# Six expert weight blocks in flight instead of four, with large SBUF buffers laid out in multiples of 512 bytes

## The chip, the cores and the metric

The kernel runs on one core of one Trainium2 chip. The metric is device time of one execution in microseconds (us). Engines are named as in the profile: PE is TensorE (PEld its weight loads), DVE is VectorE, ACT is ScalarE, POOL is GpSimd, SP is SyncE, which issues most loads.

## The reference

Two small networks run one after the other on 256 tokens of width 1024, in float32. The last and longest part is a layer of eight experts of which each token takes two:

```python
def moe(h, router, wg, wu, wd):
    logits = (h @ router).astype(jnp.float32)
    vals, idx = lax.top_k(logits, TOP_K)
    w = jax.nn.softmax(vals, axis=-1)
    gates = jnp.sum(jax.nn.one_hot(idx, N_EXPERTS, dtype=jnp.float32) * w[..., None], axis=-2)
    y = jnp.zeros_like(h)
    for e in range(N_EXPERTS):
        y = y + gates[..., e:e + 1].astype(h.dtype) * swiglu(h, wg[e], wu[e], wd[e])
    return y
...
def first_block(x, ...):
    for i in range(DEPTH):
        h = h + (moba_attention if i == 0 else rwkv7_time_mix)(rms_norm(h, norm_mix[i]), ...)
        h = h + conv_ffn(rms_norm(h, norm_ffn[i]), ...)
    return rms_norm(h, norm_final)
```

The second network (second_block) has two layers, each with modulation from a vector c, a mixer of differential attention beside a gated linear recurrence, and then a feed-forward: dense in the first layer, the experts in the second.

## The kernel before

All big weight matrices are cut on the host into blocks of 128 partitions x 2048 float32 (1 MB, 8192 bytes a partition): 162 dense blocks in the order of use, then 36 blocks for each of the 8 experts, 288 in all. A block goes through three steps. SyncE loads it into one of the RING = 4 slots of `ring`. ScalarE rounds it to float32r into one of SPLITS = 3 slots of `weights_hi` (the semaphore `hi_ready`). VectorE subtracts the rounded from the original into `weights_lo` and counts up `taken`, which lets TensorE start on the block and lets SyncE load the next one into the ring slot. TensorE multiplies hi by hi, hi by lo and lo by hi, and counts up `used`, which frees the split slot for ScalarE. So each product takes three matmuls.

The activations are split in the same way into `acts_hi` and `acts_lo`. `to_features` (L735) has a piece of the weights as its stationary operand and 256 columns of acts as the moving one: 48 matmuls a block. `to_tokens` (L746) has acts stationary and 256 columns of weights moving, 48 matmuls a block; its 12 blocks are four of the first attention, four of RWKV and two of each mixer. `project` (L766) has acts, heads or hidden values stationary and 512 columns of weights moving, 24 matmuls a block. RWKV has eight blocks of to_features and four of to_tokens.

The order on each engine is written by hand and unrolled for the dense part. The experts are a loop of seven passes and a last pass. In a pass TensorE takes six chunks of gate and up blocks (L2771, twelve 512-column matmuls a block, `xg_hi` and `xg_lo` stationary), each followed by four transposes (L2789) and two down blocks (L2814, `hT_hi` and `hT_lo` stationary). Near the end of a pass it gathers the tokens of the next expert (L2742), and near the start it scatters the results of the last one (L2754, L2756). On ScalarE `moe_hi` (L2261) rounds, on VectorE `moe_lo` (L2267) subtracts, on SyncE `load` (L2730) issues. The first four expert blocks are issued by `issue` (L340), the function of the dense ones, during the last mixer, under its wait that four blocks back has been taken.

Before the experts the router runs (L3035 to L3072): small steps between TensorE and VectorE, in which VectorE does the lower half of expert block 1 in two parts. At the very start of the kernel POOL loads the positions and the four lambda vectors; `rope_angles` and `products` on VectorE use them.

Buffers are given addresses in the order in which the program asks for them, in steps of 32 bytes, and given back at the end of a stage. Ahead of `ring` lie 16,384 bytes and four small constants in 32-byte steps, so in each partition `ring` begins at 16,512, `weights_hi` at 49,280 and `weights_lo` at 73,856, all 128 bytes past a multiple of 512. Below, the residue of a buffer is its start modulo 512. Before the change `acts_hi` begins at 153,088 (residue 0) up to the first feed-forward, at 188,064 (160) in RWKV, and at 144,896 (0) from the second feed-forward on; `hid_hi_part` has residue 0, `ada` 0, `xg_hi` and `hT_hi` 192. Each lo buffer has the residue of its hi buffer. The address table of the change follows from the sizes in the diff: a slot of `ring` is 8192 bytes, `resid`, `xn` and `AT` 8192 each, `seen` 2048.

Of the kernel before, what the change touches and what calls it, by code (L numbers as in the profile page):

```python
# [15 lines left out]
P = 128  # L16
T = 256
# [6 lines left out]
RING = 4  # L24
SPLITS = 3
# [86 lines left out]
VCOLS = _at  # L112

# [31 lines left out]
def expert_order():  # L145

    order = []
    for c in range(CHUNKS + 1):
        if c < CHUNKS:
            order += [("gate", c, 0), ("gate", c, 1), ("up", c, 0), ("up", c, 1)]  # L150
        if c:
            order += [("down", c - 1, 0), ("down", c - 1, 1)]
    assert len(order) == EXPERT_BLOCKS and EXPERT_BLOCKS % RING == 0 and EXPERT_BLOCKS % SPLITS == 0
    return order
# [59 lines left out]
def build(nc, a, out):  # L214
# [6 lines left out]
    with ExitStack() as ctx:  # L221
# [40 lines left out]
        stat = sb("stat", [P, 64])  # L262
# [7 lines left out]

        arrived = [sem(f"arrived{i}") for i in range(RING)]
        hi_ready = sem("hi_ready")
# [525 lines left out]
        seen = sb("seen", [P, TT, T])  # L798
        nlam = sb("nlam", [P, 2])
        decay8 = sb("decay8", [P, 8])  # L800
        pos_in = sem("pos_in")
# [23 lines left out]
        posq = sb("posq", [P, TT], I32, stage=heads_stage)  # L825
        fl = sb("fl", [P, 4, T], stage=heads_stage)
        cq = sb("cq", [P, TT], stage=heads_stage)
        lams = sb("lams", [P, 4, 2, DH], stage=heads_stage)
        dots = sb("dots", [P, 2, 2], stage=heads_stage)
        sp8 = sb("sp8", [P, 6, 8], stage=heads_stage)  # L830

        stages = open_joint()
        with ExitStack() as stage:
            x_in = sem("x_in")
            early_in = sem("early_in")
            norm = Norm(lambda f: v("norm_mix", f), turns=0, then=0, look=1, joined=False)
            no = norm.no
            ahead(SPLITS)
            with engine_programs() as block:
                @block.sync  # L840
                def _(sp):
                    sp.dma_start(cst[:, 0:EARLY], a["consts"][:, 0:EARLY]).then_inc(early_in, 16)
                    sp.dma_start(resid[:], a["x"][0].rearrange("(t p) d -> p t d", p=P)).then_inc(x_in, 16)
                    feed(sp, 3)
                    sp.dma_start(cst[:, EARLY:ROPE], a["consts"][:, EARLY:ROPE]).then_inc(cst_in, 16)
                    feed(sp, 5)
                    sp.dma_start(cst[:, ROPE:], a["consts"][:, ROPE:]).then_inc(cst_rest, 16)
                    feed(sp)

                @block.gpsimd  # L850
                def _(pool):
                    pool.dma_start(posb[:], a["positions_2"][0:1, :].broadcast_to([P, T])).then_inc(pos_in, 16)
                    pool.dma_start(posq[:], a["positions_2"][0].rearrange("(t p) -> p t", p=P), allow_slow_non_contiguous=True).then_inc(lams_in, 16)
                    for i, n in enumerate(("lam_q1_2", "lam_k1_2", "lam_q2_2", "lam_k2_2")):
                        pool.dma_start(lams[:, i, :, :].rearrange("p l d -> p (l d)"),
                                       a[n].rearrange("(a l) d -> a (l d)", a=1).broadcast_to([P, 2 * DH])).then_inc(lams_in, 16)

                @block.scalar
                def _(act):
                    act.dma_start(vec[:], a["vectors"]).then_inc(setup_in, 16)  # L860
# [36 lines left out]
        with ExitStack() as stage:  # L897
# [6 lines left out]
            PT += [own_PT[:, i] for i in range(2)]  # L904
            st = sb("st", [P, 8, 2, 6], stage=stage)
            heads = [sb(n, [P, KT, T], F32R, stage) for n in ("heads_hi", "heads_lo")]
# [10 lines left out]
            with engine_programs() as block:  # L917
# [129 lines left out]
                def _(dve):  # L1047
# [5 lines left out]
                    def rope_angles():  # L1053

                        dve.wait_ge(pos_in, 16)
# [99 lines left out]
                    for i in range(12):  # L1155
# [5 lines left out]
                        if i == 0:  # L1161
                            dve.wait_ge(cst_in, 16)
                            dve.wait_ge(lams_in, 80)
                            products()
# [1053 lines left out]
        open_acts(ctx)  # L2218
# [31 lines left out]
        m_xhi, m_xlo, m_hlo, m_oh, m_gc, m_st = (sem("m_" + n) for n in ("xhi", "xlo", "hlo", "oh", "gc", "st"))  # L2250
# [4 lines left out]

        def moe_hi(act, n, j):

            slot = (moe_first + j) % RING
            act.wait_ge(arrived[slot], n * (16 * EXPERT_BLOCKS // RING) + 16 * ((moe_first + j) // RING + 1))
            act.wait_ge(used, n * EXPERT_BLOCKS + (moe_first + j - SPLITS + 1))  # L2260
            nc.scalar.copy(split[0][:, (moe_first + j) % SPLITS, :], ring[:, slot, :]).then_inc(hi_ready, 1)  # L2261

        def moe_lo(dve, n, j, lo=0, hi=BLK):

            at = (moe_first + j) % SPLITS
            dve.wait_ge(hi_ready, n * EXPERT_BLOCKS + (moe_first + j + 1))
            ins = nc.vector.tensor_tensor(split[1][:, at, lo:hi], ring[:, (moe_first + j) % RING, lo:hi],  # L2267
                                          split[0][:, at, lo:hi].bitcast(F32), ALU.subtract)
            if hi == BLK:
                ins.then_inc(taken, 1)  # L2270
            else:
                dve_step.mark(ins)

        Q0, K0, X0, X1, Q1, K1, Y0, Y1, V0, V1 = range(10)
        ROTATED = (Q0, K0, Q1, K1)

        def mixer(l, no, then, norm):
# [7 lines left out]
            with ExitStack() as stage:  # L2285
                QK = sb(f"QK{l}", [P, 8, T], stage=stage)
                V = sb(f"V{l}", [P, TT, 512], stage=stage)
                xp = sb(f"xp{l}", [P, 4, T + 3], stage=stage)
# [10 lines left out]
                st = sb(f"st{l}", [P, 4, 2, 3, TT], stage=stage)  # L2299
                Pd = sb(f"Pd{l}", [P, 2, 2 * T], stage=stage)  # L2300
                PT = sb(f"PT{l}", [P, 2, 2 * T], stage=stage)
                O = raw[:].rearrange("p t (h n) -> p t h n", h=4)
# [383 lines left out]
        make_gates(1)  # L2686
        norm = Norm(gain_of(1, 0), shift(1, 0), turns=6, then=first["win1"], look=2)
        ffn(2, no, first["win1"], norm, scale=gates[0][:, 1, :], finished=1)
        router, rgain, rshift = (sb(n, [P, KT, EXPERTS]) for n in ("router", "rgain", "rshift"))
        rbias = sb("rbias", [P, EXPERTS])  # L2690
# [4 lines left out]
        slot_no = sb("slot_no", [P, 2, TT, EXPERTS])  # L2695
        gate_w = sb("gate_w", [P, TT, EXPERTS])
        info = sb("info", [1, 3 * EXPERTS], I32)
        yacc = sb("yacc", [P, TT, D])
        E = EXPERTS
        lg = sb("lg", [P, TT, E])  # L2700
        w3 = [sb(f"w3_{i}", [P, TT, E]) for i in range(5)]
        riota = sb("riota", [P, E])
        m = sb("m", [P, 8, TT])
        cn = sb("cn", [P, 4, E])
        with ExitStack() as stage:
# [3 lines left out]
            gcol = sb("gcol", [P, TT, 1], stage=stage)  # L2709
# [4 lines left out]
            oe = [sb(z, [P, D], F32R, stage) for z in ("moe_hi", "moe_lo")]  # L2714
            first_use = {key: j for j, key in enumerate(order)}
# [263 lines left out]
            with engine_programs() as block:  # L2979
                @block.sync  # L2980
                def _(sp):
                    with sp.Fori(0, E - 1) as e:
                        for j in range(RING, EXPERT_BLOCKS):
                            load(sp, e, e, j)
                        for j in range(RING):
                            sp.wait_ge(taken, e * EXPERT_BLOCKS + (EXPERT_BLOCKS + moe_first + j - RING + 1))
                            src = expert_block(e + 1, j)
                            slot = (moe_first + j) % RING
                            sp.dma_start(ring[:, slot, :], src).then_inc(arrived[slot], 16)
                    for j in range(RING, EXPERT_BLOCKS):  # L2990
# [26 lines left out]
                def _(act):  # L3017
# [8 lines left out]
                    nc.scalar.copy(ST[:].rearrange("p (a b) -> p a b", a=2), zeros(2, P)).then_inc(m_st, 1)  # L3026
# [106 lines left out]
```

## Time and profile before

| | |
|---|---|
| median of 3 runs | 2150.48 us (2148.81 to 2155.33) |
| the profiled execution | 2152.8 us, its span 2151.0 us |
| TensorE busy | 97% of the span |
| VectorE, ScalarE busy | 81%, 59% |
| mean granted TensorE clock | 0.981 of full speed |
| experts (1258.7 to about 2133 us of the span) | 288 blocks of 1 MB |
| mean HBM rate | 248 GB/s over the span, about 350 in the experts |

Busy time of TensorE is modelled at its end: matmuls overlap, so one of 512 columns shows about 395 ns though the next starts some 233 ns later. The distance from start to start, or the length of a chain piece over its count, is what tells the pace. Idle time of an engine costs only where the chain of waits passes through it.

### The profile page before, as it was taken

To read this page: it belongs to the slowest core of one execution; us is meant where nothing else is said; L and a number is where in the kernel's file an instruction comes from. 1 tells how busy PE (TensorE), PEld (TensorE's weight loads), DVE (VectorE), ACT (ScalarE), POOL (GpSimd) and SP (SyncE) were. 2 spreads that over 40 slices of the span, in tenths; PEclk is the share of its full clock that TensorE was granted. 3 is DMA by queue.
4 is the path that set the end of the run, shared out by engine and by line. 5 is a ranking of instruction groups with operands and counts; after the bars stand their busy time and mean duration, and the time that the engine had idled before them with its cause. 6 is when DMAs were issued, how large, how long until landed. Compare 5 with 4: busy or idle time off the path is not lost.

```text
span 2151.0 us, 31960 instructions
## 1 busy us (share of the span) xinstructions
PE 2087.0 (97%) x12604; PEld 1784.4 (83%) x12605; DVE 1734.9 (81%) x1995; ACT 1260.7 (59%) x1272; POOL 47.9 (2%) x83
## 2 busy tenths in 40 slices
PE   8999999998999999999999999999999999999996
PEld 7889996877789979799988878888888888888885
DVE  7758887796688878778788778988888888888886
ACT  5654444632354455753345777777677777777774
POOL 0000001000000000000000000000000000000000
PEclk9999999998799999999999999999999999999998
DMA  7358861201377644387864349898989898989894
GB/s 258 128 189 281 298 232 63 105 21 41 130 262 262 251 158 160 115 301 296 298 251 143 126 184 361 332 363 326 357 329 365 325 368 321 366 327 355 346 360 178
DMA packets 79070, 534.09 MB, mean 248 GB/s; under 512 B 11648, under 2 KB 13056, under 8 KB 15216
## 3 DMA queue, kind: packets, MB, share of 16 engines
q1 hardware_dynamic: 71440, 481.04, 60.0%
q0 software_dynamic: 7376, 51.25, 6.5%
q8 instruction: 78, 1.28, 0.2%
q14 instruction: 32, 0.26, 0.0%
q10 hardware_dynamic: 144, 0.26, 0.0%
HBM read 531.47 MB, written 1.05 MB: 248 GB/s over the span
## 4 chain that ended last, share of the span: by engine, by line
PE 86%; DVE 7%; ACT 3%; DMA 2%; issue 1%; SPq 0%; DVEq 0%; ACTq 0%
PE bank L735 25%; PE bank L2771 23%; PE bank L766 12%; PE bank L2814 11%; PE bank L746 3%; DMA ring<-in_experts 1%; PE bank L2742 1%; PE bank L409 1%; DVE weights_lo L2267 1%; PE bank L2789 1%; DVE weights_lo L373 1%; ACT weights_hi L365 1%; ACT weights_hi L2261 1%; DVE AT L2096 1%; DVE S L2095 1%
## 5 line engine op out<-in xcount | busy, mean ns | idle before, releaser
L2267 DVE TENSOR_TENSOR weights_lo<-ring,weights_hi 128x2048 fp32r<-128x2048 f32 x289 | 657.8, 2283 | 100.2 <-ACT weights_hi L2261 97.2
L2261 ACT CAST weights_hi<-ring 128x2048 fp32r<-128x2048 f32 x288 | 550.6, 1915 | 160.3 <-PE bank L2771 60.7
L735 PE MATMUL bank<-acts_hi,weights_hi 128*128 128x256 f32 x1600 | 458.1, 286 | 8.2 <-DVE acts_lo L395 4.3
L373 DVE TENSOR_TENSOR weights_lo<-ring,weights_hi 128x2048 fp32r<-128x2048 f32 x162 | 370.3, 2290 | 111.6 <-ACT weights_hi L365 110.1
L365 ACT CAST weights_hi<-ring 128x2048 fp32r<-128x2048 f32 x162 | 308.9, 1909 | 251.0 <-PE bank L735 224.2
L735 PE MATMUL bank<-acts_hi,weights_lo 128*128 128x256 f32 x1600 | 452.1, 283 | 0.0
L735 PE MATMUL bank<-acts_lo,weights_hi 128*128 128x256 f32 x1600 | 450.7, 282 | 0.0
L735 PEld LDWEIGHTS bank<-acts_hi,weights_hi 128*128 128x128 f32 x1600 | 302.0, 189 | 17.5 <-issue 12.9
L2771 PE MATMUL bank<-weights_hi,xg_hi 128*128 128x512 f32 x768 | 308.4, 402 | 1.0 <-DVE xg_lo L2890 0.4
L735 PEld LDWEIGHTS bank<-acts_lo,weights_hi 128*128 128x128 f32 x1600 | 302.2, 189 | 2.7 <-issue 1.4
L2771 PE MATMUL bank<-weights_hi,xg_lo 128*128 128x512 f32 x768 | 303.7, 395 | 0.0
L2771 PE MATMUL bank<-weights_lo,xg_hi 128*128 128x512 f32 x768 | 303.5, 395 | 0.0
L735 PEld LDWEIGHTS bank<-acts_hi,weights_lo 128*128 128x128 f32 x1600 | 301.4, 188 | 0.0
L2771 PEld LDWEIGHTS bank<-weights_hi,xg_hi 128*128 128x128 f32 x768 | 144.3, 188 | 36.4 <-DVE weights_lo L2267 2.8
L2771 PEld LDWEIGHTS bank<-weights_hi,xg_lo 128*128 128x128 f32 x768 | 144.4, 188 | 35.0
L2771 PEld LDWEIGHTS bank<-weights_lo,xg_hi 128*128 128x128 f32 x768 | 144.5, 188 | 32.3
L2814 PE MATMUL bank<-weights_hi,hT_hi 128*128 128x512 f32 x384 | 121.5, 398 | 1.8 <-DVE hT_lo L2931 1.8
L2814 PE MATMUL bank<-weights_hi,hT_lo 128*128 128x512 f32 x384 | 120.7, 395 | 0.0
L2814 PE MATMUL bank<-weights_lo,hT_hi 128*128 128x512 f32 x384 | 120.7, 395 | 0.0
L1383 DVE CUSTOM_DVE_ANT_0 ada<-ada,silu_c 128x1024 f32<-128x1024 f32 x96 | 113.5, 1220 | 0.8 <-ACT silu_c L1327 0.8
L766 PE MATMUL bank<-weights_hi,hid_hi_part 128*128 128x512 f32 x272 | 89.6, 403 | 1.5 <-DVE hid_lo_part L1370 1.5
L766 PE MATMUL bank<-weights_lo,hid_hi_part 128*128 128x512 f32 x272 | 87.4, 395 | 0.0
(467 smaller groups left out, 2743.7 us busy)
## 6 DMA issues: line engine op xcount, KB each, us to landing
ring<-in_experts SPq DMA_DIRECT2D x288, 1024.0 KB, 5.4
ring<-in_dense SPq DMA_DIRECT2D x162, 1024.0 KB, 4.9
ada<-in_ada POOLq DMA_DIRECT2D x48, 1024.0 KB, 5.1
silu_c<-in_c SPq DMA_DIRECT2D x3, 512.0 KB, 6.2
resid<-in_x SPq DMA_DIRECT2D x1, 1024.0 KB, 6.7
out<-resid SPq DMA_DIRECT2D x2, 512.0 KB, 2.6
cst<-in_consts SPq DMA_DIRECT2D x1, 649.5 KB, 9.9
kh<-in_rwkv_g SPq DMA_DIRECT2D x1, 512.0 KB, 7.1
```

The costliest lines, as they stand in the source:

```text
L365: nc.scalar.copy(split[0][:, n % SPLITS, :], ring[:, n % RING, :]).then_inc(hi_ready, 1)
L373: nc.vector.tensor_tensor(split[1][:, n % SPLITS, :], ring[:, n % RING, :], split[0][:, n % SPLITS, :].bitcast(F32), ALU.subtract).then_in ...
L409: nc.tensor.matmul(pb[bank][:], ident, const("cos", 0, 2 * T), start=True, stop=True)
L735: ins = nc.tensor.matmul(bank[:, f * T:(f + 1) * T], split[w][:, m % SPLITS, k * 256 + f * P:k * 256 + (f + 1) * P], acts[x][:, k, :], sta ...
L746: ins = nc.tensor.matmul(bank[:, t * 256:(t + 1) * 256], acts[x][:, k, t * P:(t + 1) * P], split[w][:, m % SPLITS, k * 256:(k + 1) * 256], ...
L766: ins = nc.tensor.matmul(pb[4 + 2 * t + h][:], src[x][:, tile + f, t * P:(t + 1) * P], split[w][:, m % SPLITS, f * D + h * 512:f * D + (h ...
L1383: ins = nc.vector.tensor_tensor_reduce(out=w, in0=w, in1=silu_c[:], op0=ALU.mult, op1=ALU.add, scale=1.0, scalar=0.0, accum_out=mods[:, l, ...
L2095: L(tt(o, N[:, w:, j:w].broadcast_to([P, n, w]), Z[:, j:w, 0:w].broadcast_to([P, n, w]), ALU.mult))
L2261: nc.scalar.copy(split[0][:, (moe_first + j) % SPLITS, :], ring[:, slot, :]).then_inc(hi_ready, 1)
L2267: ins = nc.vector.tensor_tensor(split[1][:, at, lo:hi], ring[:, (moe_first + j) % RING, lo:hi], split[0][:, at, lo:hi].bitcast(F32), ALU.s ...
L2771: ins = nc.tensor.matmul(bank[:], xp[x][:, 4 * half + k, :], split[w][:, slot, k * 512:(k + 1) * 512], start=(half == 0 and k == 0 and w + ...
L2814: ins = nc.tensor.matmul(pb[6 + b][:], hT[x][:, c % 2, q * P:(q + 1) * P], split[w][:, slot, f * D + b * 512:f * D + (b + 1) * 512], start ...
```

## The change

Six blocks are in flight in the experts. The two new ring places, `ring_more`, lie where the split activations lay, which are given back after the last mixer; SyncE loads into them once TensorE has used the last dense block. `place(j)` gives the buffer and the semaphore of block j: its index modulo DEEP = 6, the first four in the old ring, two in the new one. The small tensors (constants, vectors, statistics, router terms) are gathered into a few pieces, `small`, `few`, `routing` and `kept`, whose sizes are multiples of 512 bytes, and buffers of odd size come last in their stage. `make_gates(1)` takes its memory earlier. The semaphores `pos_in` and `m_st` are dropped: their instructions count on `lams_in` and `m_oe`, and the waits are raised to match.

```diff
 RING = 4
+MORE = 2
+DEEP = RING + MORE
...
+SMALL = 2944
...
-        mods = sb("mods", [P, 2, 48])
-        gain2 = sb("gain2", [P, 2, 2, KT])
-        cst = sb("cst", [P, CONSTS.shape[1]])
-        vec = sb("vec", [P, VCOLS])
         resid = sb("resid", [P, TT, D])
         xn = sb("xn", [P, TT, D])
         AT = sb("AT", [P, KT, T])
-        stat = sb("stat", [P, 64])
+        seen = sb("seen", [P, TT, T])
+        small = sb("small", [P, SMALL])
...
+        cst, vec, stat = piece(CONSTS.shape[1]), piece(VCOLS), piece(64)
+        mods = piece(96).rearrange("p (l n) -> p l n", l=2)
...
         posb = sb("posb", [P, T], I32, stage=heads_stage)
-        posq = sb("posq", [P, TT], I32, stage=heads_stage)
         fl = sb("fl", [P, 4, T], stage=heads_stage)
-        cq = sb("cq", [P, TT], stage=heads_stage)
         lams = sb("lams", [P, 4, 2, DH], stage=heads_stage)
-        dots = sb("dots", [P, 2, 2], stage=heads_stage)
-        sp8 = sb("sp8", [P, 6, 8], stage=heads_stage)
+        few = sb("few", [P, P], stage=heads_stage)
...
-                        dve.wait_ge(pos_in, 16)
+                        dve.wait_ge(lams_in, 96)
...
-        bonus = sb("bonus", [P, TT, HEADS], stage=rwkv)
         S0 = sb("S0", [P, KT, DH], stage=rwkv)
-        fac = sb("fac", [P, KT], stage=rwkv)
...
         make_gates(0)
-        open_acts(ctx)
+        make_gates(1)
+        routing = sb("routing", [P, 3 * P])
...
+        split_acts = ExitStack()
+        open_acts(split_acts)
...
+        def place(j):
+
+            i = j % DEEP
+            if i < RING:
+                slot = (moe_first + i) % RING
+                return ring[:, slot, :], arrived[slot], 16 * ((moe_first + i) // RING)
+            return ring_more[0][:, i - RING, :], arrived_more[i - RING], 0
+
         def moe_hi(act, n, j):
 
-            slot = (moe_first + j) % RING
-            act.wait_ge(arrived[slot], n * (16 * EXPERT_BLOCKS // RING) + 16 * ((moe_first + j) // RING + 1))
+            src, sem_in, earlier = place(j)
+            act.wait_ge(sem_in, n * (16 * EXPERT_BLOCKS // DEEP) + (earlier + 16 * (j // DEEP + 1)))
             act.wait_ge(used, n * EXPERT_BLOCKS + (moe_first + j - SPLITS + 1))
...
+        split_acts.close()
+        ring_more[0] = sb("ring_more", [P, MORE, BLK])
+        kept = sb("kept", [P, P])
...
             def load(sp, e, n, j):
 
-                src = expert_block(e, j)
-                slot = (moe_first + j) % RING
-                sp.wait_ge(taken, n * EXPERT_BLOCKS + (moe_first + j - RING + 1))
-                sp.dma_start(ring[:, slot, :], src).then_inc(arrived[slot], 16)
+                dst, sem_in, _ = place(j)
+                sp.wait_ge(taken, n * EXPERT_BLOCKS + (moe_first + j - DEEP + 1))
+                sp.dma_start(dst, expert_block(e, j)).then_inc(sem_in, 16)
...
                 if t == 0:
-                    pe.wait_ge(m_st, 1)
-                    pe.wait_ge(m_oe, s * 2 + 2)
+                    pe.wait_ge(m_oe, s * 2 + 3)
...
                 def _(sp):
+                    sp.wait_ge(used, moe_first)
+                    for j in range(RING, DEEP):
+                        dst, sem_in, _ = place(j)
+                        sp.dma_start(dst, expert_block(0, j)).then_inc(sem_in, 16)
                     with sp.Fori(0, E - 1) as e:
-                        for j in range(RING, EXPERT_BLOCKS):
+                        for j in range(DEEP, EXPERT_BLOCKS):
                             load(sp, e, e, j)
```

## Rows read from the trace of the kernel before

**Rows 1.** The page: busy time of TensorE, its granted clock, DMA by slices.
```profile
PE 2087.0 (97%) x12604; PEld 1784.4 (83%) x12605; DVE 1734.9 (81%) x1995; ACT 1260.7 (59%) x1272; POOL 47.9 (2%) x83
...
PEclk9999999998799999999999999999999999999998
DMA  7358861201377644387864349898989898989894
```

**Rows 2.** The chain that ended last, experts: start us, length us, what.
```profile
1359.82 3.57 PE bank L2742 x32
1363.39 5.60 PE bank L2814 x24
...
1387.88 0.44 PE bank L2789 x4
...
1468.92 3.57 PE bank L2742 x32
...
2015.84 3.57 PE bank L2742 x32
```

**Rows 3.** The same chain where it leaves TensorE, first stretch.
```profile
1536.88 7.60 DMA ring<-in_experts
...
1544.58 1.92 ACT weights_hi L2261
...
1546.53 2.30 DVE weights_lo L2267
```

**Rows 4.** Waits from 1250 us on: total us, times, longest us.
```profile
DVE weights_lo L2267 <- ACT weights_hi L2261: 97.2, 157, 1.6
...
ACT weights_hi L2261 <- DMA ring<-in_experts: 52.0, 56, 2.3
...
PEld bank L2771 <- DVE weights_lo L2267: 2.8, 6, 0.7
```

**Rows 5.** Timeline of SyncE and TensorE around the last projection: start us, us.
```profile
1234.02 0.36 SPq L2730 DMA_DIRECT2D ring<-in_experts  x1
...
1255.10 0.34 SPq L2730 DMA_DIRECT2D ring<-in_experts  x1
...
1240.05 0.39 PE L766 MATMUL bank<-weights_hi,acts_lo 128*128 128x512 f32 x1
```

**Rows 6.** Timeline of POOL and VectorE at the start, and the landings of lams.
```profile
4.26 0.57 POOL L855 DMA_DIRECT2D lams<-in_lam_k  x1
...
23.37 0.49 DVE L1083 TENSOR_TENSOR lams<-lams 128x128 f32<-128x128 f32 x2
...
DMA to landing us min/median/max: 7.1/7.6/9.0
```

**Rows 7.** Groups of VectorE by form: count, then busy us, mean ns of one.
```profile
L1370 DVE TENSOR_TENSOR hid_lo_part<-hf,hid_hi_part 128x512 fp32r<-128x512 f32 x34 | 23.5, 692 | 20.0 <-ACT hid_hi_part L1324 20.0
...
L395 DVE TENSOR_TENSOR acts_lo<-mix,acts_hi 128x512 fp32r<-128x512 f32 x12 | 7.5, 685 | 1.5 <-ACT acts_hi L389 1.5
```

**Rows 8.** The page's DMA issues: count, KB each, median us to landing.
```profile
ring<-in_dense SPq DMA_DIRECT2D x162, 1024.0 KB, 4.9
ada<-in_ada POOLq DMA_DIRECT2D x48, 1024.0 KB, 5.1
```

**Rows 9.** The chain in two dense feed-forward stretches.
```profile
206.79 11.52 PE bank L735 x96
218.31 5.58 PE bank L766 x24
...
1035.13 11.39 PE bank L735 x96
```

**Rows 10.** Timeline of TensorE in RWKV; 13 such rows lie between these.
```profile
366.27 0.28 PE L735 MATMUL bank<-acts_lo,weights_hi 128*128 128x256 f32 x1
...
367.91 0.28 PE L735 MATMUL bank<-acts_hi,weights_hi 128*128 128x256 f32 x1
```

**Rows 11.** The page's groups: to_features, one of its three operand pairs.
```profile
L735 PE MATMUL bank<-acts_hi,weights_hi 128*128 128x256 f32 x1600 | 458.1, 286 | 8.2 <-DVE acts_lo L395 4.3
```

More of the change, by code:

```diff
@@ L152, in expert_order @@
             order += [("down", c - 1, 0), ("down", c - 1, 1)]
-    assert len(order) == EXPERT_BLOCKS and EXPERT_BLOCKS % RING == 0 and EXPERT_BLOCKS % SPLITS == 0
+    assert len(order) == EXPERT_BLOCKS and EXPERT_BLOCKS % DEEP == 0 and EXPERT_BLOCKS % SPLITS == 0
     return order
@@ L261, in build, with piece @@
         AT = sb("AT", [P, KT, T])
-        stat = sb("stat", [P, 64])
+        seen = sb("seen", [P, TT, T])
+        small = sb("small", [P, SMALL])
+        at_small = [0]
+        def piece(n):
+            at_small[0] += n
+            assert at_small[0] <= SMALL
+            return small[:, at_small[0] - n:at_small[0]]
+        cst, vec, stat = piece(CONSTS.shape[1]), piece(VCOLS), piece(64)
+        mods = piece(96).rearrange("p (l n) -> p l n", l=2)
+        gain2 = piece(4 * KT).rearrange("p (l i k) -> p l i k", l=2, i=2)
+        nlam, decay8, fac = piece(2), piece(8), piece(KT)
+        bonus = piece(TT * HEADS).rearrange("p (t h) -> p t h", t=TT)
         def const(name, lo=0, n=None):
@@ L271, in build @@
         arrived = [sem(f"arrived{i}") for i in range(RING)]
+        arrived_more = [sem(f"arrived_more{i}") for i in range(MORE)]
         hi_ready = sem("hi_ready")
@@ L904, in build @@
             PT += [own_PT[:, i] for i in range(2)]
+            heads = [sb(n, [P, KT, T], F32R, stage) for n in ("heads_hi", "heads_lo")]
             st = sb("st", [P, 8, 2, 6], stage=stage)
-            heads = [sb(n, [P, KT, T], F32R, stage) for n in ("heads_hi", "heads_lo")]
             sc = DH ** -0.5
@@ L2217, in build @@
         make_gates(0)
-        open_acts(ctx)
+        make_gates(1)
+        routing = sb("routing", [P, 3 * P])
+        router, rgain, rshift = (routing[:, 64 * i:64 * i + 64].rearrange("p (k e) -> p k e", k=KT) for i in range(3))
+        rbias, riota = routing[:, 192:200], routing[:, 200:208]
+        by_tile = lambda i: routing[:, 208 + 16 * i:224 + 16 * i].rearrange("p (t e) -> p t e", t=TT)
+        lg, w3, m = by_tile(0), [by_tile(1 + i) for i in range(5)], routing[:, 304:320].rearrange("p (i t) -> p i t", t=TT)
+        cn = routing[:, 320:352].rearrange("p (i e) -> p i e", e=EXPERTS)
+        split_acts = ExitStack()
+        open_acts(split_acts)
         no = norm_turn(lambda f: v("norm_ffn", KT + f), turns=3, then=ffn_plan[1]["gate", 0], look=2)
@@ L2249, in build @@
         m_t, m_ht, m_oe, m_sc, m_y = (sem("m_" + n) for n in ("t", "ht", "oe", "sc", "y"))
-        m_xhi, m_xlo, m_hlo, m_oh, m_gc, m_st = (sem("m_" + n) for n in ("xhi", "xlo", "hlo", "oh", "gc", "st"))
+        m_xhi, m_xlo, m_hlo, m_oh, m_gc = (sem("m_" + n) for n in ("xhi", "xlo", "hlo", "oh", "gc"))
         routed = sem("routed")
@@ L2266, in moe_lo @@
             dve.wait_ge(hi_ready, n * EXPERT_BLOCKS + (moe_first + j + 1))
-            ins = nc.vector.tensor_tensor(split[1][:, at, lo:hi], ring[:, (moe_first + j) % RING, lo:hi],
+            ins = nc.vector.tensor_tensor(split[1][:, at, lo:hi], place(j)[0][:, lo:hi],
                                           split[0][:, at, lo:hi].bitcast(F32), ALU.subtract)
@@ L2272, in moe_lo @@
                 dve_step.mark(ins)
+        ring_more = [None]
         Q0, K0, X0, X1, Q1, K1, Y0, Y1, V0, V1 = range(10)
@@ L2714, in build @@
             oe = [sb(z, [P, D], F32R, stage) for z in ("moe_hi", "moe_lo")]
+            gcol = sb("gcol", [P, TT, 1], stage=stage)
             first_use = {key: j for j, key in enumerate(order)}
@@ L2981, in _ @@
                 def _(sp):
+                    sp.wait_ge(used, moe_first)
+                    for j in range(RING, DEEP):
+                        dst, sem_in, _ = place(j)
+                        sp.dma_start(dst, expert_block(0, j)).then_inc(sem_in, 16)
                     with sp.Fori(0, E - 1) as e:
-                        for j in range(RING, EXPERT_BLOCKS):
+                        for j in range(DEEP, EXPERT_BLOCKS):
                             load(sp, e, e, j)
[L2985 to L2990, printed above, removed]
+                        for j in range(DEEP):
+                            dst, sem_in, _ = place(j)
+                            sp.wait_ge(taken, e * EXPERT_BLOCKS + (EXPERT_BLOCKS + moe_first + j - DEEP + 1))
+                            sp.dma_start(dst, expert_block(e + 1, j)).then_inc(sem_in, 16)
+                    for j in range(DEEP, EXPERT_BLOCKS):
                         load(sp, E - 1, E - 1, j)
@@ L3025, in _ @@
                         nc.scalar.copy(z[:].rearrange("p (a b) -> p a b", a=2), zeros(2, D // 2)).then_inc(m_oe, 1)
-                    nc.scalar.copy(ST[:].rearrange("p (a b) -> p a b", a=2), zeros(2, P)).then_inc(m_st, 1)
+                    nc.scalar.copy(ST[:].rearrange("p (a b) -> p a b", a=2), zeros(2, P)).then_inc(m_oe, 1)
                     all_passes(act, act_pass)
```

35 lines of the change are left out of this document (13 added, 22 removed).

## The prediction

> **What bounds the kernel now.** I read the page first: TensorE is busy for 97% of the span, and in the second half, where the experts run, the 16 DMA engines alternate between 8 and 9 tenths of busy time [rows 1]. So either TensorE or the weight stream could be the limit of the part that the ring change aims at, and the shares don't say which. The chain of waits does. It runs through the experts on TensorE alone, with pieces of 24 matmuls in 5.60 us (two weight blocks, so 2.80 us a block), except in two stretches, near 1530 and near 1955, where it goes round a loop of weight DMA, ScalarE rounding and VectorE subtraction [rows 2, 3]. Waits say what that is worth. ScalarE waits for a landing 56 times, 52.0 us in all; VectorE waits for ScalarE for 97.2 us; but TensorE's weight loads wait for VectorE's lower halves only 6 times, 2.8 us in total [rows 4]. SyncE issues each load as soon as VectorE frees its slot, so the slots set when it starts. So the loads are often late for ScalarE and almost never for TensorE, and TensorE's queue is what ends last.
>
> The length of a pass confirms it. Gathers start at 1359.82 and 1468.92, 109.10 us apart [rows 2]. By the pieces, 36 blocks x 2.80 = 100.8 us, six transposes x 0.44 = 2.6, the gather 3.57, and the eight scatter matmuls with two transposes (ten steps of at most 0.233, so about 2.1) make 109.1. Nothing is left for a wait in a normal pass. The six passes from 1359.82 to 2015.84 took 656.02 us, and six normal ones would be 654.60: 1.4 us were lost in six passes, in the stretches where the chain leaves TensorE [rows 2, 3].
>
> **The ring.** The change has up to six loads in flight instead of four. In a stalled stretch a load took 7.60 us from issue to landing, then 1.92 of ScalarE and 2.30 of VectorE before its slot was free: 11.8 us around the loop for four blocks, 2.95 a block, against TensorE's 2.80 [rows 3]. With six slots the same loop allows 1.97 a block. So the loop can't close on TensorE, unless the landing time grows in step. If the engines were moving data as fast as they can, it would: the loads then share one rate, and queueing two more only lengthens each. The stalls are short, though, and over a pass the demand (36 MB in 109.1 us) is met at four slots. I take the lost time as won back: **-1.4 us**. The bound above is -2.8 (all that TensorE waited for VectorE), the bound below 0. What ScalarE gains of its 52 us buys nothing; what is late next for it is a free split slot, which TensorE gives back at its own pace.
>
> **The start of the ring.** SyncE now waits until TensorE has used the last dense block (its last projection ends at 1240.3), then issues blocks 4 and 5, and behind them queues block 6, which could have gone at 1234. Before, block 4 was issued at 1234.02 and the next only at 1255.10, since VectorE frees slots slowly during the routing [rows 5]. With some 4.9 us to land, blocks 4 and 5 are there by about 1248, and the fifth block is first wanted after 1270, so this costs nothing; if the cover were gone it would be 6 us once. In the first pass the waits are for ScalarE and VectorE, which have the zeroing, a table load and the gather's work to do, so earlier loads don't shorten it.
>
> **Semaphores.** The angle computation now waits for all six small POOL loads. The last is issued at 4.26 and needs at most 9.0 us; VectorE first reads them at 23.4 and only then, behind other work, turns to the angles [rows 6]. Nothing. The merge of m_st into m_oe lets the first scatter wait for the same ScalarE instruction as before; moving gates, router terms and small tensors moves no instruction. Zero for all.
>
> **The addresses: the part that can matter.** The words say multiples of 512. Worked out from the sizes, the big buffers come to lie at 128 bytes past one, because the ring itself starts there: 98,432 + 3 x 8192 + 2048 + 11,776 = 136,832 = 267 x 512 + 128, and everything after that in whole multiples of 512. The split weights stay where they are, also at 128. What moves is the partner of the weights in each matmul: acts go from residue 0 (160 in the RWKV stage) to 128, the experts' xg and hT from 192 to 128. So relative to the weights the partner goes from 128 away (32 in RWKV, 64 in the experts) to 0.
>
> Does that show in the trace? For VectorE and loads no: a 128x512 subtraction takes 692 ns into residue 0 and 685 into 160 [rows 7], and 1 MB lands in 5.1 us at residue 0 (ada) and in 4.9 at 128 (the ring) [rows 8]. For TensorE it does. Steps of 256 columns, all at the full granted clock [rows 1]: 96 in 11.52 us (120.0 ns) or in 11.39 (118.6) with acts at 0, but in RWKV, with acts at 160, fourteen steps in 367.91 - 366.27 = 1.64 us, 117.1 ns [rows 9, 10]. Within a stretch the step is constant, whatever VectorE and DMA do beside it, so I read it as a matter of operands. Steps of 512 columns: 24 in 5.58 us (232.5 ns) with the partner at 0, 24 in 5.60 (233.3) in the experts [rows 2, 9]. No row has the two operands at the same residue. This is the unknown cost.
>
> The Trainium skill speaks against any effect: the page "SBUF — State Buffer", section "Specifications (TRN2)", gives SBUF 16-byte cachelines, and all starts before and after are multiples of 32. By it the steps would stay as they are and this part would be 0. The trace disagrees at least in that 160 and 0 differ by 2 to 3 ns.
>
> How I choose: if the pattern repeats every 64 or 128 bytes, distance 0 equals distance 128, which is today's dense case. That seems likelier than a period so long that 0 and 128 differ. Then the 256-column steps outside RWKV (1600 x 3 steps of to_features [rows 11] and 12 blocks x 48 of to_tokens, less 12 blocks x 48 in RWKV, so 4800) keep 118.6 to 120, mean about 119.3: 0, with +3.4 or -3.4 us if they all fell into one of the two. RWKV's 576 steps go from 117.1 to 119.3: **+1.3 us**. The experts' 288 x 12 = 3456 steps go from 233.3 to 232.5: **-2.8 us**.
>
> **Sum.** -1.4 + 1.3 - 2.8 = -2.9 us on the profiled execution's 2152.8 (span 2151.0 and 1.8 around it). That execution lies 2.3 above the median of the runs shown, 2150.5, so the forecast is 2150.5 - 2.9 = **2147.6 us**. Its own range, with 3.4 either way for the two dense steps, 2.8 if the experts don't get quicker, and the stall's bounds, is 2143 to 2154.
>
> **Rivals.**
> 1. *Equal residues are like RWKV's 32.* Then the 4800 dense steps go from 119.3 to 117.1, -10.6 us; RWKV and experts 0, stalls -1.4: 2138.5 us. For it: 32 is the nearest distance to 0 that a row has. Against: a pattern that repeats every 64 or 128 bytes. Chance 0.22.
> 2. *Equal residues are the worst case: both operand streams hit the same place together.* Taken as far above 120 as RWKV's step is below it, 123 ns, 4800 x 3.7 + 576 x 5.9 = +21 us, with -1.4: 2170 us. From +7.9 us in the steps (1.5 ns each over 5376) it decides for slower. For it: no row excludes it, and TensorE has no slack anywhere to hide it. Against: in no seen case is the mean above 120. Chance 0.12.
> 3. *Nothing at all.* The loads were limited by their rate in the two stalls, and every step stays as it is, RWKV's and the experts' included, because what set RWKV apart was not its addresses: 2150.5 us. It lies inside the forecast's range; chance 0.2 of the 0.62 below. The cacheline rule of "SBUF — State Buffer" in the Trainium skill gives the same time.
> 4. *The stalls weigh more in ordinary runs than in the profile.* The three runs differ by 6.5 us; if that were all late weights, six slots would bring 2147 and less. Chance 0.04, toward 2143.
>
> **Numbers.** A measurement of this kernel tells about 0.3%, 6.5 us, from no change. The forecast with rival 3 has 0.62, nearly all of it within; rival 1 is faster; rival 2 is slower two times in three; the edges of the forecast's class (all dense steps at 118.6 and no stall) reach below 2144 about one time in eight. That makes faster 0.31, same 0.58, slower 0.11. The range 2138 to 2156 holds the forecast's class and rival 1 and leaves rival 2 out.
>
> **What the profile of the changed kernel would show.** Ring: ScalarE's wait for in_experts falls from 52.0 us to a few, no DMA piece in the experts' chain, all gathers 109.1 apart or less, landing times longer. Start: two loads issued near 1240. Addresses: the 96-step pieces at 11.4 to 11.5 (forecast), 11.2 (rival 1), 11.8 (rival 2); 24 matmuls of the experts in 5.58; RWKV's steps at 119. VectorE's and ScalarE's durations unchanged. The prediction would be wrong if the 256-column step left 118.6 to 120, or if deeper loads slowed TensorE's own reading.

## The result, and the profile after

The changed kernel takes 2132.91 us (median of 5, 2132.15 to 2136.18) against 2149.46 us before; the ratio is 0.9924, interval 0.9914 to 0.9935. It is 16.5 us faster. The forecast was 2147.6 us with a range of 2138 to 2156: the way was right, the size was not, and rival 1, the quickest case named, stopped at 2138.5 for the wrong reason.

The profiled execution took 2132.15 us, its span 2130.3. The chain that ended last, in an ordinary part of the experts and then in a dense feed-forward stretch and at RWKV's start (start us, length us, what; L749 is to_features, L780 project, L2787 and L2830 the experts' two forms):

```profile
1389.02 5.44 PE bank L2830 x24
1394.46 5.44 PE bank L2787 x24
...
206.81 11.51 PE bank L749 x96
218.32 5.47 PE bank L780 x24
...
365.26 23.28 PE bank L749 x192
```

Here lies the answer. Two expert blocks take 5.44 us where they took 5.60 [rows 2]: 226.7 ns a matmul of 512 columns instead of 233.3. The dense 512-column matmuls go from 5.58 to 5.47 us for 24, and 96 matmuls of 256 columns stay at 11.51, the slower of their two paces [rows 9]. RWKV's start takes 23.28 / 192 = 121.3 ns a matmul, starting cost included; once started it runs at 120.0 where it ran at 116.7.

The waits from 1230 us on (total us, times, longest us):

```profile
DVE weights_lo L2292 <- ACT weights_hi L2286: 82.0, 151, 1.3
ACT weights_hi L2286 <- PE bank L2787: 79.7, 121, 1.3
ACT weights_hi L2286 <- PE bank L2830: 57.8, 72, 0.8
...
PEld bank L2787 <- DVE weights_lo L2292: 3.6, 8, 0.7
```

The wait of ScalarE for in_experts (52.0 us, [rows 4]) is gone, and ScalarE waits longer for TensorE instead. That is what the ring of six does. The expected longer landing did not come: a load of an expert block lands after 5.2 us in `ring` and 5.5 in `ring_more` (medians), against 5.4 before. TensorE's own wait for lower halves did not fall: 3.6 us instead of 2.8. It now comes in every pass at the same place, where VectorE has the scattered results to add (start us, us; the number after the form is a count):

```profile
1379.26 1.40 DVE L2924 SCALAR_TENSOR_TENSOR yacc<-bank,gcol,yacc 128x512 f32<-128x512 f32 x2
1380.80 0.17 DVE L2930 COPY gcol<-kept 128x2 f32 x1
1380.92 4.49 DVE L2292 TENSOR_TENSOR weights_lo<-ring,weights_hi 128x2048 fp32r<-128x2048 f32 x2
```

TensorE starts its next block only at 1383.27, when the first of these two subtractions is done. Its four transposes start at 1382.52, so 0.75 us pass from their start to the block's; at the same place in the kernel before, and after other transposes now, it is 0.35. With quicker matmuls this stretch of VectorE work is late by 0.4 us.

The start of the ring went as forecast. SyncE issues the two new loads, one behind the other, from 1237.96 on and block 6 at 1239.17:

```profile
1237.96 0.81 SPq L3001 DMA_DIRECT2D ring_more<-in_experts  x2
1239.17 13.75 SPq L2750 DMA_DIRECT2D ring<-in_experts  x2
```

### The profile page after: what moved, and what is told of

Read it like the earlier page. It is cut to its first block, busy times and chain, and to the rows that moved or that the text cites. A ratio compares the mean times of both kernels' runs of the same rounds, so it can differ in the third digit from the quotient of the medians.

```text
span 2130.3 us, 31979 instructions
## 1 busy us (share of the span) xinstructions
PE 2062.8 (97%) x12604; PEld 1785.9 (84%) x12605; DVE 1732.2 (81%) x1995; ACT 1260.1 (59%) x1272; POOL 48.1 (2%) x83
## 4 chain that ended last, share of the span: by engine, by line
PE 81%; DVE 9%; ACT 5%; issue 4%; DMA 1%; ACTq 0%; DVEq 0%; SPq 0%
PE bank L749 26%; PE bank L2787 19%; PE bank L780 12%; PE bank L2830 11%; PE bank L760 3%; ACT weights_hi L2286 3%; PE bank L423 1%; DVE weights_lo L2292 1%; PE bank L2805 1%; DVE weights_lo L387 1%; ACT weights_hi L379 1%; DVE AT L2105 1%; DVE S L2104 1%; DMA ring<-in_dense 1%; DVE yacc L2924 0%
## 5 line engine op out<-in xcount | busy, mean ns | idle before, releaser
L2292 DVE TENSOR_TENSOR weights_lo<-ring,weights_hi 128x2048 fp32r<-128x2048 f32 x193 | 437.7, 2280 | 70.9 <-ACT weights_hi L2286 70.5
L749 PE MATMUL bank<-acts_hi,weights_hi 128*128 128x256 f32 x1600 | 458.6, 287 | 9.0 <-DVE acts_lo L538 4.7
L387 DVE TENSOR_TENSOR weights_lo<-ring,weights_hi 128x2048 fp32r<-128x2048 f32 x162 | 370.3, 2290 | 111.0 <-ACT weights_hi L379 109.6
L379 ACT CAST weights_hi<-ring 128x2048 fp32r<-128x2048 f32 x162 | 308.8, 1909 | 249.7 <-PE bank L749 224.6
L749 PE MATMUL bank<-acts_lo,weights_hi 128*128 128x256 f32 x1600 | 452.6, 283 | 0.0
L749 PE MATMUL bank<-acts_hi,weights_lo 128*128 128x256 f32 x1600 | 452.5, 283 | 0.0
L2286 ACT CAST weights_hi<-ring 128x2048 fp32r<-128x2048 f32 x192 | 367.9, 1917 | 76.1 <-PE bank L2787 46.4
L749 PEld LDWEIGHTS bank<-acts_hi,weights_hi 128*128 128x128 f32 x1600 | 306.7, 192 | 18.2 <-issue 12.9
L749 PEld LDWEIGHTS bank<-acts_lo,weights_hi 128*128 128x128 f32 x1600 | 306.8, 192 | 2.5 <-issue 1.4
L749 PEld LDWEIGHTS bank<-acts_hi,weights_lo 128*128 128x128 f32 x1600 | 306.8, 192 | 0.0
L2787 PE MATMUL bank<-weights_hi,xg_hi 128*128 128x512 f32 x768 | 303.9, 396 | 1.9 <-DVE weights_lo L2292 1.3
L2787 PE MATMUL bank<-weights_hi,xg_lo 128*128 128x512 f32 x768 | 299.6, 390 | 0.0
L2787 PE MATMUL bank<-weights_lo,xg_hi 128*128 128x512 f32 x768 | 299.1, 389 | 0.0
L2292 DVE TENSOR_TENSOR weights_lo<-ring_more,weights_hi 128x2048 fp32r<-128x2048 f32 x96 | 218.7, 2288 | 12.2 <-ACT weights_hi L2286 11.5
L2286 ACT CAST weights_hi<-ring_more 128x2048 fp32r<-128x2048 f32 x96 | 183.2, 1916 | 65.5 <-PE bank L2787 33.4
L2787 PEld LDWEIGHTS bank<-weights_hi,xg_hi 128*128 128x128 f32 x768 | 144.3, 188 | 33.9 <-DVE weights_lo L2292 3.6
L2787 PEld LDWEIGHTS bank<-weights_hi,xg_lo 128*128 128x128 f32 x768 | 144.1, 188 | 30.8
L2787 PEld LDWEIGHTS bank<-weights_lo,xg_hi 128*128 128x128 f32 x768 | 144.3, 188 | 28.3
L2830 PE MATMUL bank<-weights_hi,hT_hi 128*128 128x512 f32 x384 | 119.8, 393 | 1.8 <-DVE hT_lo L2947 1.8
L2830 PE MATMUL bank<-weights_hi,hT_lo 128*128 128x512 f32 x384 | 118.9, 391 | 0.0
L2830 PE MATMUL bank<-weights_lo,hT_hi 128*128 128x512 f32 x384 | 118.7, 390 | 0.0
L1394 DVE CUSTOM_DVE_ANT_0 ada<-ada,silu_c 128x1024 f32<-128x1024 f32 x96 | 113.5, 1220 | 0.8 <-ACT silu_c L1338 0.8
```

The costliest lines, as they stand in the source:

```text
L379: nc.scalar.copy(split[0][:, n % SPLITS, :], ring[:, n % RING, :]).then_inc(hi_ready, 1)
L387: nc.vector.tensor_tensor(split[1][:, n % SPLITS, :], ring[:, n % RING, :], split[0][:, n % SPLITS, :].bitcast(F32), ALU.subtract).then_in ...
L749: ins = nc.tensor.matmul(bank[:, f * T:(f + 1) * T], split[w][:, m % SPLITS, k * 256 + f * P:k * 256 + (f + 1) * P], acts[x][:, k, :], sta ...
L1394: ins = nc.vector.tensor_tensor_reduce(out=w, in0=w, in1=silu_c[:], op0=ALU.mult, op1=ALU.add, scale=1.0, scalar=0.0, accum_out=mods[:, l, ...
L2286: nc.scalar.copy(split[0][:, (moe_first + j) % SPLITS, :], src).then_inc(hi_ready, 1)
L2292: ins = nc.vector.tensor_tensor(split[1][:, at, lo:hi], place(j)[0][:, lo:hi], split[0][:, at, lo:hi].bitcast(F32), ALU.subtract)
```

## The experiments

Each ratio is to the kernel before, run on the same chip beside the variant. For the variants with the old kernel's experts moved, with four slots and with everything moved its median was 2151.33 us, for the last two kernels below 2150.67. Distance means, throughout, how far the start of the non-weight operand (acts, xg, hT) lies beyond that of the weights, modulo 512.

**TensorE by itself, different distances.** The first probe has no other engine at work.

> Nothing of the reference is computed: TensorE alone runs 90 stretches of float32r matmuls in the kernel's own order of operands (hi x hi, hi x lo, lo x hi), 48 with 256 moving columns (weights stationary, or acts stationary) or 24 with 512 columns, with the start of acts moved by 0 to 480 bytes against that of the weights, or both moved together, or the weights alone. Distance theory (the difference of the two operands' starts modulo 512 sets the step): 512 columns 226.7 ns at distance 0 and 232 to 233.4 at 64 and 128; 256 columns 120 ns at 0, 117 at 32, 118.6 to 120 at 128; both moved together gives the same as distance 0. Rival, own start (what counts is where acts themselves begin): both moved together by 32 or 64 bytes gives the steps of acts moved alone. Rival, outside cause (VectorE, ScalarE or DMA traffic slows the reads): all stretches alike, since nothing else runs.

Means from start to start, the first gap of each stretch left out. With weights stationary and 256 columns moving: 119.9 ns at distance 0, 116.7 at 32, 117.8 at 64, 113.4 at 192, and the same again 256 bytes further on (113.5 at 448). With both operands moved together by 32, 64, 128 or 256 bytes the 256-column steps are those of distance 0. With 512 columns moving it is 228.0 ns at distance 0, 233.2 at 64 and 232.4 at 128, and 226.7 to 228.6 with both moved together. The stretches of 512 columns at distance 0, at 32 and at 64 in the chain (24 matmuls each, starting cost included):

```profile
384.68 5.53 PE bank L66 x24
...
390.27 5.64 PE bank L66 x24
...
395.97 5.64 PE bank L66 x24
```

So it is the distance that counts, not where an operand begins; over the distances tried it repeats every 256 bytes; and no other engine is needed for it. My pattern of 64 or 128 bytes does not exist. One distance was run twice and gave two paces: 256 columns at 128 took 118.6 ns, and 120.0 when it came again after a stretch at distance 0. The dense stretches of the kernel before, all at 128 but RWKV's, have just these two paces.

**The kernel before, only the experts' operands moved.**

```diff
         with ExitStack() as stage:
+            sb("pad", [P, 112], stage=stage)
             xg = sb("xg", [P, KT, P], stage=stage)
```

> The kernel before with 448 unused bytes ahead of xg in the experts' stage, so that xg, hT and moe_hi begin at 128 past a multiple of 512 like the weights; ring of four and everything else as it was. Operand theory: the experts' step of 512 columns falls from 233.3 to 226.7 ns, 3456 steps, -22.8 us at most; with four slots the loop of DMA, ScalarE and VectorE (2.95 us a block when it stalled) then closes more often on a block of 2.72 us, so I expect -14 to -22 us, 2128 to 2136. Ring theory (the gain of the change came from six slots): no change, 2149.

2141.13 us, ratio 0.9945 (0.9923 to 0.9966). One unused buffer of 448 bytes makes the old kernel 10 us faster, with four slots and all addresses outside the experts' stage as they were. Its experts step at the new pace, but it wins less than the 14 to 22 us expected: TensorE is now quick enough to meet the ring, and its passes (from gather to gather) take between 106.8 and 109.3 us where the changed kernel's take 106.9. Its waits from 1270 us on:

```profile
ACT weights_hi L2261 <- DMA ring<-in_experts: 66.9, 69, 2.5
...
PEld bank L2772 <- DVE weights_lo L2267: 7.8, 15, 1.2
```

TensorE's weight loads wait 7.8 us for lower halves where the kernel before waited 2.8 [rows 4].

**The changed kernel with four slots.**

```diff
-DEEP = RING + MORE
+DEEP = RING
```

> The changed kernel with DEEP = RING, all else with its new addresses: four blocks in flight. Operand theory: within a few us of the changed kernel, slower by 1 to 8 us (2134 to 2141), with TensorE waiting for lower halves more often than 8 times. Ring theory: back to 2149.

2138.75 us (2135.86 to 2148.06), ratio 0.9951 (0.9934 to 0.9969), against 0.9924 (0.9914 to 0.9935) with six. The two extra slots are worth about 6 us at the new pace, though the intervals touch at their ends. The next variant, run beside it with six slots, took 2127.70 to 2134.02 us, clear of all these times. The profile agrees: four of its passes take 107.3 to 109.6 us instead of 106.9, 5.5 us in all, and in three of the four the chain goes round the loop of load, rounding and subtraction. The wait for in_experts is back, and with it TensorE's:

```profile
ACT weights_hi L2286 <- DMA ring<-in_experts: 60.9, 70, 2.7
...
PEld bank L2787 <- DVE weights_lo L2292: 8.1, 17, 1.4
```

Two of the loads in its chain:

```profile
1509.91 7.46 DMA ring<-in_experts
1521.88 7.68 DMA ring<-in_experts
```

They start 11.97 us apart, 2.99 a block.

**Weights and partners moved together.**

```diff
+        sb("pad", [P, 16])
         ring = sb("ring", [P, RING, BLK])
```

> The changed kernel with 64 unused bytes ahead of the ring, so that weights and partners all begin at 192 past a multiple of 512. Distance theory: the same as the changed kernel within 2 us (2133), 512-column steps 226.7 ns. Own-start theory (128 is a good start and 192 a bad one): the experts' steps return to 233, about +20 us, 2153.

2132.33 us, ratio 0.9907 (0.9886 to 0.9928), the changed kernel's time. All large buffers now begin at 192 past a multiple of 512, where the experts' partners had begun in the slow kernel, and the pace is the fast one. The words "multiples of 512" name no cause; equal starts modulo 256 do.

**The changed kernel with six slots, the experts' partners back at distance 64.**

```diff
         with ExitStack() as stage:
+            sb("pad", [P, 16], stage=stage)
             xg = sb("xg", [P, KT, P], stage=stage)
```

> The changed kernel with 64 unused bytes ahead of xg in the experts' stage: six slots, but the experts' stationary operands again 64 bytes beyond the weights, as before the change. If the ring of six were worth much by itself, this would keep most of the gain. Distance theory: the experts' 3456 steps go back to 233.2 ns, +22 us against the changed kernel, 2150 to 2155, and what remains against the kernel before is the ring at slow steps (-1.4) and the dense part (512 columns quicker by 5 ns x 1200, 256 columns slower by 0.9 ns x 5400, about -1).

2149.53 us, ratio 0.9995 (0.9984 to 1.0005). Sixty-four unused bytes take the whole gain away, with six blocks in flight. The chain has its old pieces back, and TensorE's weight loads wait for lower halves only twice:

```profile
1441.64 5.60 PE bank L2788 x24
1447.24 5.60 PE bank L2831 x24
```

```profile
PEld bank L2788 <- DVE weights_lo L2292: 0.8, 2, 0.4
```

The deeper ring at the old pace, together with all that the new addresses do to the dense part, is worth nothing that can be measured. The profile shows the little that it does:

```profile
1361.43 3.57 PE bank L2760 x32
...
2015.95 3.57 PE bank L2760 x32
```

The six passes between these gathers take 654.52 us and none is longer than 109.10, where the kernel before needed 656.02 [rows 2].

**The changed kernel with acts at the best distance for 256 columns.**

```diff
-        def open_acts(stage):
+        def open_acts(stage, apart=True):
 
+            if apart:
+                sb("pad", [P, 48], stage=stage)
             acts[:] = [sb(n, [P, KT, T], F32R, stage) for n in ("acts_hi", "acts_lo")]
+            if apart:
+                sb("pad", [P, 16], stage=stage)
```

> The changed kernel with 192 unused bytes ahead of acts_hi and 64 behind acts_lo (not in RWKV's first stage), so that acts begin 64 bytes before the weights' start modulo 256, the best distance for 256 columns in the probe (steps of about 113.4 ns against 119.9). Distance theory: 4416 steps of to_features save 6.5 ns each, 28.7 us, 384 steps of to_tokens 2.2 ns each, 0.8 us, and the 288 steps of project with acts lose 1.2 ns each; about -29 us against the changed kernel, 2104 (2100 to 2112 if ScalarE and VectorE begin to hold TensorE up). Rival (in the full kernel other traffic, not the distance, sets the step of 256 columns): no change, 2133.

2120.94 us (2119.31 to 2122.27), ratio 0.9861 (0.9843 to 0.9879): 12 us better than the changed kernel, the best version run, but not the 29 us expected. The chain shows where the rest stayed. It is in the first dense feed-forward, then in a feed-forward stretch a little later, then in a mixer:

```profile
143.25 22.26 PE bank L753 x192
...
204.46 11.31 PE bank L753 x96
...
1153.87 5.66 PE bank L753 x48
```

These are 115.9, 117.8 and 117.9 ns by the piece, but they are not alike. In the first and the third the first matmuls are slow to start, and the rest run at 113.3 ns to the end. Twelve steps near the end of the first piece take 1.36 us:

```profile
163.76 0.28 PE L753 MATMUL bank<-acts_lo,weights_hi 128*128 128x256 f32 x1
...
165.12 0.28 PE L753 MATMUL bank<-acts_lo,weights_hi 128*128 128x256 f32 x1
```

The second runs at 117.8 from its first matmul to its last. So it is with all 52 stretches of to_features at this distance: each keeps one pace once it is under way. All 23 that directly follow matmuls of `project` have 117.8; of the 29 others, 20 have 113.3 and 9 have 117.8. That makes 2880 of 4416 steps that are 4.5 ns slower than the probe's, 13 of the missing 17 us. The gain is real, and the probe's 113.4 is had only in a third of the steps.

**Two more probes.**

> Nothing of the reference is computed: TensorE alone, as in the first probe, but with the starts of weights_lo, acts_hi and acts_lo moved one by one by 0, 64, 128 or 192 bytes (64 combinations each for 256 columns with weights stationary and for 512 columns with acts stationary), then acts moved by odd multiples of 16 bytes and by a few steps near 192. Distance theory in its simple form: each step depends on the distance between its own two operands, or on that between a matmul's moving operand and the next matmul's stationary one, and the best combinations are those with all distances best: 113.4 ns for 256 columns at -64, 226.7 for 512 at 0; no combination beats both. Rival: hi and lo interact, and some mixed combination is quicker than any equal one.

The simple form failed, and so did the rival's hope of more. For 256 columns the two quickest of the 64 combinations were mixed ones: 113.5 ns with weights_lo moved by 128 bytes and both acts by 64, and 114.2 with weights_lo and both acts moved by 192. Of their three pairs of operands only one, and two, stand at -64. The combination with hi and lo alike at 192, which had given 113.4 in the first probe, took 117.8 here from start to end. What is known to differ is the stretch before it; the chip was another too, but the kernel above ran on that chip and has both paces. The chain has the equal one at 192 and the quickest mixed one (48 matmuls each):

```profile
123.34 5.71 PE bank L59 x48
```

```profile
250.38 5.51 PE bank L59 x48
```

Moving both acts by 112 bytes gave 113.3, a second good place, so no mixed combination went below the best equal one. For 512 columns acts moved by 144 bytes gave 226.7, distance 0 gave 227.3, and the quickest mixed combination 227.8. So equal hi and lo are as good as any, and 226.7 stood as a floor in all that I tried.

> Nothing of the reference is computed: TensorE alone, now with the kernel's own four forms (to_features, to_tokens, an experts' gate block pair, an experts' down block pair) with their accumulation and their banks, at distances 0 to 224 bytes in steps of 32, upwards and then downwards again. Distance theory: to_features 120 at 0, 117.8 at 32, 113.4 at 192; both experts' forms 226.7 at 0 and 233.3 at 64, as in the kernels. Rival for the 117.8 instead of 113.4 ns in most dense stretches of the kernel with acts at -64 (the accumulation or the banks slow them): 117.8 at 192 here too. Against it (the state in which a stretch is entered chooses between two steps at one distance): both 113.4 and another value at 192, upwards and downwards.

Means in ns from start to start, worked out from its trace with the first three gaps of each stretch left out; two numbers where the way up and the way down differ by more than 0.5:

```
distance, bytes            0      32          64     96           128    160          192    224
to_features, 256       120.0  116.7/117.9  117.8  120.0        118.8  117.3        113.5  118.4
to_tokens, 256         119.9  118.3        113.5  117.3/120.0  118.8  120.0        117.8  116.8
gate pair, 512         228.2/227.2  233.2  233.3  234.3        232.4  233.1        228.9  233.3
down pair, 512         227.2  233.2        233.3  234.3        232.4  233.2        228.8  233.3
```

The table gives the paces of the kernels: the dense to_features of the kernel before stood at distance 384, which is 128 modulo 256 (118.8); RWKV's at 32 (116.7 and 117.9); the experts at 64 before (233.3) and at 0 after (227.2). It is read with the sign turned for to_tokens, where acts are stationary. It also shows that one distance can have two paces (to_features at 32, to_tokens at 96). At 192 to_features had 113.3 going up and 113.6 going down. So accumulation and banks are not what slows the kernel with acts at -64. The probe before this one had 117.8 at the same distance with TensorE alone, so no other engine is needed for the slow pace either. What went before a stretch is then the likely cause, but the state that carries it over was not found.

The chain of this probe shows three of the table's cells as pieces: to_features at 0 and at 192, and the gate pair at 32.

```profile
37.63 5.81 PE bank L56 x48
...
72.39 5.50 PE bank L56 x48
...
227.89 5.64 PE bank L67 x24
```

## Why the prediction was wrong

*What bounds the kernel.* Right, and it decided everything: TensorE's queue ends last, so a step of TensorE that shrinks shows almost in full.

*The ring, -1.4 us.* Its mechanism was right: with the experts at their old pace six slots are worth no measurable time (ratio 0.9995), and in the profiles the six passes are 1.5 us shorter. What was missed is that its worth depends on the pace. At 2.72 us a block the loop of four, 2.95 when it stalls, binds more often, and six slots are then worth about 6 us. The two parts of the change are not a sum of two separate terms: moving the experts alone gave 10 us, and the slots gave most of the rest. The new dense addresses show in none of these comparisons: with fast experts and four slots the ratio is 0.9945 without them and 0.9951 with them, and with slow experts it is 0.9995 with them and six slots.

*The start of the ring, the semaphores.* Nothing, as said; the loads were issued from 1237.96 on, and no wait for an expert load is left in the list.

*The addresses.* The reading of the trace was right (the step follows the two operands' addresses, and RWKV differs for that reason), and the fact that decides it was stated: no row had both operands at one residue. (The 2 to 3 ns between 160 and 0 are 1.5 to 2.9 by its own rows.) The step that failed is "How I choose": I took distance 0 to equal distance 128, on a pattern of 64 or 128 bytes. The pattern is 256 bytes. For 256 columns that cost little, since TensorE alone needs 120.0 ns at 0 and 118.6 or 120.0 at 128. For 512 columns it was the whole error: 227 ns at 0, 232.4 at 128. The term it mis-sized is the experts' 512-column step: forecast 232.5 ns, -2.8 us; measured 226.7 in the chain, -23.0 us. The dense 512-column steps had no term of their own, because the rule gave them 0; they came to -5.5 us. Rival 1 failed in the same place, since it gave the experts 0 and expected its gain from 256 columns. For those I had +1.3 us in RWKV and 0 elsewhere; all settled at the slow pace of 120. That the way was right owes something to luck: the forecast had the experts quicker by 2.8 us for a reason that did not hold.

The sum with measured pieces, from the chains of both profiles:

```
experts, 144 pieces of 24:  144 x (5.44 - 5.60)            = -23.0
dense 512 columns, 50 of 24: 50 x (5.47 - 5.58)            =  -5.5
dense 256 columns: 4800 x (119.9 - 119.3) ns               =  +2.9
RWKV 256 columns:  3 x (23.28 - 22.66)                     =  +1.9
stalls of the ring won back                                =  -1.4
```

That is -25.1 us, against 2130.3 - 2151.0 = -20.7 in the spans. Most of the difference lies in the experts' passes. The gathers of this profile start at 1355.05 and 1461.95:

```profile
1355.05 3.74 PE L2759 MATMUL bank<-Sel,xn 128*128 128x128 f32 x32
...
1461.95 3.74 PE L2759 MATMUL bank<-Sel,xn 128*128 128x128 f32 x32
```

They are 106.90 us apart. The 18 pieces of a pass should have brought 109.10 - 18 x 0.16 = 106.22, so 0.68 us a pass is lost again, 5.4 us in eight. The late subtraction at 1383 is 0.4 of it. The other 0.3 is in the pieces of 24 that come right after transposes or the gather, seven in a pass: from start to start they take 5.56 to 5.59 us, 0.12 to 0.15 above the new 5.44, where they took 5.68 or 5.69, 0.08 or 0.09 above the old 5.60. With these 5.4 us the sum is -19.7; the last microsecond, which the dense part won beyond its terms, I have not assigned.

*The Trainium skill's cachelines.* The page "SBUF — State Buffer", section "Specifications (TRN2)", gives 16-byte cachelines, and I read from it that starts at multiples of 32 can't differ. The probe shows 113.4 to 120.0 and 227.2 to 234.3 ns for such starts. The measurement decides: the rule says nothing of the distance between a matmul's two operands, and that is what the step followed.

## What to carry to other kernels

When TensorE's queue ends last and the operands are float32r, compute the distance of the two start addresses modulo 256 for every large matmul before the change and after it. A few unused bytes ahead of a buffer moved this kernel by 10 to 17 us either way, more than two extra blocks in flight did. For float32r and 512 columns the same start modulo 256 was the best of the 32-byte steps; for 256 columns measure the distance with TensorE alone first, and then look in the kernel's own trace how many stretches keep the pace. And where a change moves addresses, run the version with its named effect and the old distances before believing the name: here that version had no gain at all. When the cost of a case that no row shows is the unknown, take the widest relative spread that any form shows and apply it to every form, in both directions. Here the 256-column rows spread from 117.1 to 120.0 ns, 2.5%; 2.5% of 233 ns over the experts' 3456 steps is 20 us, close to the 23 that came.

## What the runs showed of the hardware

The pace of a float32r matmul depends on the distance between the starts of its moving and stationary operands, repeats every 256 bytes over the distances tried, and does so with all other engines idle: 226.7 to 228.2 ns for 512 columns at distance 0 and 233.1 to 233.4 at 32 or 64; 120 ns for 256 columns at 0 and 113.4 where the moving operand begins 64 bytes before the stationary one. Both are at the full granted clock (1.00 in the probes and in the stretches of the kernels read here). Four bytes are enough: with acts 4 bytes beyond the weights 256 columns took 123.1 ns, the slowest of all.

VectorE's and ScalarE's durations did not follow the addresses. The subtraction into `hid_lo_part` took 692 ns at residue 0 and 693 at 128, the rounding into `hid_hi_part` 621 ns at both; with all weight buffers moved from 128 to 192 the weights' subtraction stayed at 2290 ns.

At some distances there are two paces: 113.3 and 117.8 ns at 192, 118.6 and 120.0 at 128, 116.7 and 117.8 at 32 (256 columns, weights stationary). In the profiles looked at, a stretch without a pause keeps the one it has once under way. The same dense part at the same addresses can get either: the first dense feed-forward ran at 120.0 ns in the profile of the kernel before and at 118.6 in that of the old kernel with its experts moved. What sets it is open, and so is whether the chip has a part in it.
